# State space mixer: first inputs loaded during the output linear, a second Toeplitz buffer, the scale product inside the chain, the root spread by TensorE, states first

## The reference

```python
def rmsnorm(x, g):
    y = xf * lax.rsqrt(jnp.mean(xf * xf, axis=-1, keepdims=True) + EPS)
    return y.astype(x.dtype) * g
...
x = x + gate * y            # odd_mix: y = (...) @ w_out
return rmsnorm(x, final_g)
...
# s5_mixer: 64 groups of 16 channels, 64 complex states each
bu_re = jnp.einsum('blgh,gph->lbgp', u, bb_re)
bu_im = jnp.einsum('blgh,gph->lbgp', u, bb_im)
_, _, s_re, s_im = lax.associative_scan(
    _ssm_combine, (a_seq_re, a_seq_im, bu_re, bu_im), axis=0)
y = (jnp.einsum('lbgp,ghp->blgh', s_re, c_re) - jnp.einsum('lbgp,ghp->blgh', s_im, c_im))
y = y.reshape(bsz, seq, D_MODEL) + d_skip * x
h = jax.nn.gelu(y)
val, gate = jnp.split(h @ w_glu, 2, axis=-1)
z = val * jax.nn.sigmoid(gate)
return (z @ w_out).astype(x.dtype)
```

## Time and profile before

| | us |
|---|---|
| median of 3 runs | 4361.92 |
| lowest and highest | 4359.04, 4365.49 |
| the profiled execution | 4365.49 |
| its span | 4363.6 |
| TensorE busy | 4080.8 (94%) |
| VectorE, ScalarE, GpSimd busy | 2007.1 (46%), 1271.8 (29%), 1308.2 (30%) |

### The profile page before, as it was taken

The page is one execution under the profiler, slowest core; times in us unless marked ns, Lnnn a source line. Parts: engine busy times, 40 slices in busy tenths (PEclk is TensorE's granted clock), DMA queues, the critical chain, the costliest instruction groups (busy, mean ns, idle before and its releaser), DMA issues.

```text
span 4363.6 us, 51384 instructions
## 1 busy us (share of the span) xinstructions
PE 4080.8 (94%) x20067; PEld 3122.6 (72%) x20067; DVE 2007.1 (46%) x2419; ACT 1271.8 (29%) x1884; POOL 1308.2 (30%) x780
## 2 busy tenths in 40 slices
PE   7999998899999999779999999999999899999998
PEld 5776774458777774568888888876666678888886
DVE  4264662765676775561453233324444554323322
ACT  3122320212222221231232232224545543223222
POOL 1530000021111110012344444443344444444443
PEclk8999999999999999899999999999999999999999
DMA  6111004331222223751223333321000032333333
GB/s 230 39 37 55 0 0 143 139 131 64 73 79 73 79 86 131 162 139 49 81 92 97 99 98 96 100 88 68 25 20 25 20 107 92 96 98 100 96 97 105
DMA packets 120619, 372.02 MB, mean 85 GB/s; under 512 B 18004, under 2 KB 35727, under 8 KB 116688
## 3 DMA queue, kind: packets, MB, share of 16 engines
q1 hardware_dynamic: 102496, 300.84, 22.1%
q0 software_dynamic: 11584, 55.30, 3.4%
q10 hardware_dynamic: 6384, 13.70, 0.8%
HBM read 329.37 MB, written 38.06 MB: 84 GB/s over the span
## 4 chain that ended last, share of the span: by engine, by line
PE 62%; issue 17%; DVE 8%; POOL 6%; DMA 3%; ACT 2%; SPq 1%; POOLq 0%; ACTq 0%; DVEq 0%
PE banks L274 22%; PE banks L3037 6%; POOL w_parts L259 6%; PE banks L1227 5%; PE banks L288 5%; PE banks L693 5%; PE banks L1602 4%; PE banks L979 3%; PE banks L3111 2%; DVE neg_max L1058 2%; PE banks L3140 1%; PE banks L3127 1%; PE banks L1583 1%; DMA w_ring<-in_weights 1%; PE banks L1633 1%
## 5 line engine op out<-in xcount | busy, mean ns | idle before, releaser
L259 POOL TENSOR_TENSOR w_parts<-w_ring,w_parts 128x1024 fp32r<-128x1024 f32 x344 | 835.5, 2430 | 1143.3 <-ACT w_parts L252 1143.3
L274 PE MATMUL banks<-x_high,w_parts 128*128 128x512 f32 x2944 | 912.3, 390 | 0.0
L252 ACT ACTIVATE w_parts<-w_ring 128x1024 fp32r<-128x1024 f32 x344 | 364.5, 1060 | 1298.1 <-PE banks L274 1280.8
L274 PEld LDWEIGHTS banks<-x_high,w_parts 128*128 128x128 f32 x2944 | 552.6, 188 | 116.8 <-issue 2.1
L274 PE MATMUL banks<-x_low,w_parts 128*128 128x512 f32 x1472 | 572.8, 389 | 0.0
L274 PE MATMUL banks<-hidden_high,w_parts 128*128 128x512 f32 x1600 | 482.3, 391 | 6.0 <-POOL w_parts L259 6.0
L3245 DVE TENSOR_TENSOR_SCAN arena<-arena,flags 128x128 f32<-128x128 f32 (+3 forms) x192 | 229.6, 1200 | 285.7 <-ACT arena L3186 284.3
L274 PEld LDWEIGHTS banks<-hidden_high,w_parts 128*128 128x128 f32 x1600 | 301.8, 189 | 70.9 <-POOL w_parts L259 6.8
L2929 DVE TENSOR_TENSOR hidden_high<-banks,gate_temps 128x512 f32 (+1 forms) x88 | 60.9, 692 | 571.9 <-PE banks L274 571.8
L274 PEld LDWEIGHTS banks<-x_low,w_parts 128*128 128x128 f32 x1472 | 276.3, 188 | 59.2 <-issue 1.9
L1227 PE MATMUL banks<-parts_b,w_ring_low 128*128 128x512 f32 x896 | 303.9, 406 | 14.5 <-DVE resid_low L391 9.7
(11 more groups left out here) (448 smaller groups left out, 6495.6 us busy)
## 6 DMA issues: line engine op xcount, KB each, us to landing
w_ring<-in_weights SPq DMA_DIRECT2D x488, 512.0 KB, 3.5
arena<-in_hy_dft SPq DMA_DIRECT2D x11, 1536.0 KB, 6.1
s_cl<-arena POOLq DMA_DIRECT2D x4, 1152.0 KB, 5.4
arena<-s_cl POOLq DMA_DIRECT2D x4, 1152.0 KB, 7.0
resid<-in_xT ACTq DMA_DIRECT2D x2, 2048.0 KB, 25.9
resid<-in_xT POOLq DMA_DIRECT2D x1, 4096.0 KB, 13.7
arena<-in_fn_seq POOLq DMA_DIRECT2D x1, 4096.0 KB, 18.0
resid_spill<-resid POOLq DMA_DIRECT2D x1, 4096.0 KB, 12.6
```

Source lines behind the costliest of these rows:

```text
L252: nc.scalar.activation(WP[:, g % 2, 0, :], WR[:, (g % RING) * TILE:(g % RING + 1) * TILE], ACT.Identity).then_inc(w_hi, 1)
L259: nc.gpsimd.tensor_tensor(WP[:, g % 2, 1, :], WR[:, (g % RING) * TILE:(g % RING + 1) * TILE], WP[:, g % 2, 0, :].bitcast(F32), ALU.subtrac ...
L274: mm = nc.tensor.matmul(PS[:, bank + h // H, :], w[a][:, k % KB, :], srcs[b][:, k, at + h:at + h + H], start=(first and i + q == 0), stop= ...
```

## The change

- Quarter 0 of the inputs is loaded into its own place `U0` by GpSimd during the output linear, as soon as it has been written to `u_dram`; `normed(0)` reads it from there. SyncE begins with `inputs_in(1)`. `U0` shares its place with `STT_`, whose first column VectorE now clears.
- The Toeplitz matrices get a second buffer `TP[1]`, at the place of HT's last two blocks, cleared once the spill has landed. Toeplitz copies run up to one quarter ahead. A third powers buffer `CLS[2]` lies in HT too, `CLS[3]` is `CLS[1]` again.
- `normed(q+1)` stands inside `chain(q)`, behind the four products that read the banks.
- The taps move ahead on TensorE (`taps`): quarter 0 around the token sums in `OdOut`, quarter 1 behind `states_in(0)`, quarter 2 behind `results(0)`, quarter 3 ahead of `results(2)`. ScalarE's order follows.
- The last square is added on VectorE, so TensorE sums one tensor. The sums of all tokens and their roots for `RINV` go away; `spread_rows` spreads `RINV8` over the partitions by 8 matmuls within `results(3)`, and ScalarE copies them into `RINV`.
- GpSimd brings back the results of quarters 0 to 2; SyncE issues half of the last result copy, ScalarE the other half; the residual comes back after the last result.

```diff
+    CLS += [HT_[:, 3840:6144].rearrange(cl_shape["pattern"], i=2, j=QP, n=9), CLS[1]]
-    TP = ar(27136, 2048, "p (g n) -> p g n", g=16)
+    TP = [t.rearrange("p (g n) -> p g n", g=16) for t in (ar(27136, 2048), HT_[:, 6144:8192])]
+    U0 = ar(25072, 2048, "p (g c) -> p g c", g=16)
...
 OdOut.pool
-            nc.gpsimd.memset(TP, 0.0).then_inc(s5_zero, 1)
-            nc.gpsimd.memset(STT_, 0.0).then_inc(s5_zero, 1)
+            nc.gpsimd.memset(TP[0], 0.0).then_inc(s5_zero, 1)
+            g.wait_ge(u_out, 16)
+            for t in range(CK):
+                g.dma_start(U0[16 * t:16 * t + 16], u_dram[0:2 * P, t, :].rearrange("(g h) c -> h g c", h=16)
+                            ).then_inc(s5_e, 16)
...
 OdOut.pe
+            wait_done(p, OdOut.done)
+            S5.taps(p, 0, range(4))
             p.wait_ge(s5_vbt, 4)
             p.wait_ge(s5_zero, 2)
...
+            OdOut.waits(p, "sq_free", 7)
+            for t in range(CK):
+                mm = nc.tensor.matmul(PS[:, 4, 0:NC], PARTS_OF_ONES[:, 112 - 16 * t:240 - 16 * t], ACC_SQ[:, t:T:CK],
+                                      start=(t == 0), stop=(t == CK - 1))
+            mm.then_inc(n_sem["spread_in"], 1)
+            S5.taps(p, 0, range(4, QP))
...
 S5.sp
             def toeplitz(q):
                 s.wait_ge(s5_km, 4 * (q + 1))
+                s.wait_ge(s5_zero, 3 if q == 0 else 5)
+                if q > 1:
+                    s.wait_ge(s5_y, 4 * (q - 1))
                 if q:
-                    s.wait_ge(s5_y, 4 * q)
+                    s.wait_ge(s5_tp, 16 * CK * q)
                 for t in range(CK):
...
-            inputs_in(0)
+            inputs_in(1)
             inputs_out(3)
...
             toeplitz(0)
-            s.wait_ge(spilled, 80)
+            inputs_in(2)
+            toeplitz(1)
+            inputs_in(3)
             for q in range(4):
                 s.wait_ge(s5_ye, 4 * (q + 1))
...
+                    s.wait_ge(y_out, 16 * CK * q)
+                for t in range(CK if q < 3 else CK // 2):
+                    S5.result_out(s, q, t)
+                if q < 2:
+                    toeplitz(q + 2)
+            s.wait_ge(y_out, 16 * CK * 4)
+            s.dma_start(HT[:, 6:8, :], y_dram[6 * P:8 * P].rearrange("(k p) t c -> p k (t c)", p=P)).then_inc(x_home, 16)
+            s.wait_ge(x_home, 16)
             s.dma_start(XT, spill).then_inc(x_home, 16)
...
 S5.pool
             magnitudes(0)
+            g.wait_ge(spilled, 80)
+            g.wait_ge(s5_r, 8)
+            powers_in(2)
+            nc.gpsimd.memset(TP[1], 0.0).then_inc(s5_zero, 1)
             g.wait_ge(s5_vt, 8)
             magnitudes(1)
...
+            g.wait_ge(s5_st, 1)
+            phases_in(2)
+            magnitudes(2)
+            result_in(0)
+            g.wait_ge(s5_st, 2)
+            phases_in(3)
+            magnitudes(3)
+            g.wait_ge(s5_y, 8)
+            powers_in(3)
+            result_in(1)
+            result_in(2)
...
 S5.chain
             nc.vector.memset(FLAG[:, 0:1], 0.0).then_inc(s5_vr, 1)
+            if q < 3:
+                S5.normed(v, q + 1)
...
 S5.dve
-            normed(0)
-            normed(1)
-            v.wait_ge(s5_zero, 4)
+            S5.normed(v, 0)
+            v.wait_ge(s5_un, 1)
+            link(nc.vector.memset(STT_[:, :, :, 0:1], 0.0))
             v.wait_ge(u_out, 64)
...
 S5.act
             kernels(0)
...
+            kernels(1)
+            for q in range(3):
+                S5.turned_out(a, q + 1)
+                if q == 2:
+                    kernels(3)
                 results(q)
...
+                if q == 0:
+                    kernels(2)
+            a.wait_ge(s5_st, 3)
+            for k in (0, 1):
+                high(k)
+            a.wait_ge(s5_v, 4)
+            a.wait_ge(s5_tp, 16 * CK * 4)
+            for j in (-2, -1):
+                round_ahead(a, PLAN["glu"], j)
+            for k in (2, 3):
+                high(k)
+            OdOut.waits(a, "spread_in", 2)
+            nc.scalar.activation(RINV[:, :].rearrange("p (c t) -> p t c", t=CK),
+                                 PS[:, 0:2, :].rearrange("p b (t c) -> p (b t) c", c=NC),
+                                 ACT.Identity).then_inc(n_sem["root"], 1)
+            results(3)
             a.wait_ge(s5_ye, 16)
+            a.wait_ge(y_out, 16 * CK * 3)
+            for t in range(CK // 2, CK):
+                S5.result_out(a, 3, t)
             for k in range(4, KB):
                 high(k)
...
 S5.pe
-            OdOut.waits(p, "root", 3)
             states_in(0)
-            wait_done(p, OdOut.done)
-            kernels(0)
+            S5.taps(p, 1, range(QP))
             for q in range(4):
                 if q < 3:
                     p.wait_ge(s5_vr, q + 1)
                     S5.turned(p, q + 1)
                     states_in(q + 1)
+                if q == 2:
+                    S5.taps(p, 3, range(QP))
                 results(q)
-                if q < 3:
-                    kernels(q + 1)
+                if q == 0:
+                    S5.taps(p, 2, range(QP))
```

More of the change, by code:

```diff
@@ L2233, in act @@
                                  ).then_inc(n_sem["root"], 1)
-            OdOut.waits(a, "mean_in", 1)
-            for h in range(2):
-                nc.scalar.activation(RINV[:, h * H:(h + 1) * H], PS[:, 6 + h, :], ACT.Sqrt, scale=1.0 / D,
-                                     bias=EPS(RMS_EPS)).then_inc(n_sem["root"], 1)
         def dve(v, link):
@@ L2255, in _build @@
     S.append(OdOut)
[L2256 removed]
+    for _key, _n in (("sq_ready", 8), ("sq_free", 7), ("spread_in", 2), ("root", 2), ("scaled", KB)):
         n_count[_key] += _n
@@ L2429, in dve @@
                 low(k)
-            OdOut.waits(v, "root", 3)
-            link(nc.vector.reciprocal(RINV[:, :], RINV[:, :]))
-            v.wait_ge(x_home, 16)
+            OdOut.waits(v, "root", 2)
+            v.wait_ge(x_home, 32)
             for k in range(KB):
```

168 lines of the change are left out of this document (75 added, 93 removed).

## The result

| | before | after |
|---|---|---|
| median, us | 4363.57 (4 runs, 4359.04 to 4365.49) | 4333.98 (4 runs, 4331.79 to 4335.03) |
| ratio after to before | | 0.9933, 95% interval 0.9916 to 0.9950 |
| the profiled execution, its span | 4365.49, 4363.6 | 4331.79, 4329.7 |

The change saves 29.6 us by the medians, 0.68%. The forecast was 37.3 us less, 4324.6 us, with a range of 4313 to 4338. The result lies in that range, but above the 4319 to 4331 that the prediction gave to its main theory.

A forecast was written before the change was run, and what follows sets the result against it. No engine is busy throughout the mixer's 150 us; head, middle and tail carry it. Savings of 11.0 + 11.1 + 14.5 + 0.7 = 37.3 us take the median 4361.92 to 4324.6 us, range 4313 to 4338.

The forecast's parts named there:

- main theory: The summed forecast for the mixer stage, with (c) included: total of 4319 to 4331 us, chance 0.66.
- (a): Middle of the mixer: DMA engines or SyncE bound the quarters, which stay at 26.4 us; 12.6 us more, 4337; chance 0.14.
- (d): ScalarE closes a circle, evicting taps q only after Toeplitz copy q-1 lands: 38.7 us a quarter, total 4374; chance 0.03.
- (e): Head: U0 lands after the output linear; up to 11 us less gained, 4336; chance 0.04 together with smaller losses.
- (c): TensorE is late at the low clock, 26.9 us a quarter against 22.2; +4.7 us, 4329; counted within the forecast's 0.66.
- (b): Chain 0 starts earlier, divided issue saves 2.7 us: 4319, down to 4314 if the tail's blocks pass sooner; chance 0.12.
- Start of chain 0: Head: early U0 load lets chain 0 start once the last inputs land, 1790.7 instead of 1801.7; 11.0 us saved.
- the slack that I gave ScalarE: Head: ScalarE's wait for Toeplitz copy 0, landing by 1792 to 1797, costs nothing, with 10 us to the next chain.
- The four chains: Middle: VectorE's four chains run back to back, 86.3 us against 97.4; 11.1 us saved.
- End of the chains to the last GELU: Behind the last chain only the state part of results 3 and GELUs are left; 14.5 us saved.
- the term "5.1 us": Time from the last chain's end to the last GELU, with a handover, against 19.6 us before.
- The tail: Last GELU to the reload's issue: ScalarE issues four of eight copies; 0.7 us saved, 2.7 if issuing takes the time.

The follow-up runs named there:

- the late load: Changed kernel, but GpSimd loads quarter 0 into U0 only after the output linear has ended, ahead of the spill; stage 149.36 us, total 4335.86 us.
- the first experiment: Changed kernel, but GpSimd waits for the end of the last chain before making the low weight parts of the GLU's first tiles; stage 139.03, total 4331.67 us.
- the combined kernels: Changed kernel with late spill, late GpSimd weight parts, 4 useless matmuls, earlier input evictions: 4322.28 us; second also puts quarter 2's taps behind its states: 4322.89 us.

## Why the prediction was right, and where not

**Direction and range** came out as forecast, the size 6.4 us too large in the stage (30.85 against 37.3). The mechanism of each step is in the trace: the late landing at the head, chains back to back, the Toeplitz copy off the tail, the reload 6.4 us behind the last GELU. Rivals (a), (d) and (e) didn't happen: no chain waited for states, ScalarE closed no circle. That the total, 4334.0, lies near the 4337 of (a) is chance, and direction and range alone don't show the terms right. Of (c) only the low clock ahead of the last GELU came, and not because TensorE was late. The hope of (b) that the last blocks pass sooner without the 4 MB reload beside them did not come true: they took 8.45 us before and 8.43 after.

**Start of chain 0**, 9.5 instead of 11.0: the step that takes the landing over as 16.4 us was mis-sized, it took 18.2. What decides was named rightly: the spill moved away brings it 7.4 us earlier. The spill is not all of it, as the late load shows (19.7 us). That the place of `normed(1)` costs and saves nothing by itself was right within 0.3 us. The slack that I gave ScalarE was wrong: Toeplitz copy 0 landed so that the eviction ran at 1800.57, not by 1792 to 1797, because I took the 7 us of an issue in free queues for one in the crowd, 13.25 us. States 1 ended at 1810.5 and chain 0 at 1811.9; 1.4 us of slack were left of my 10.

**The four chains**, 90.0 instead of 86.3: the step that failed is "back to back", a sum over VectorE's own durations with nothing beside it. I had checked who waits for the chain, not what runs next to it. The change moves GpSimd's two subtractions of the GLU's weight parts, which were long behind the chains (1907.7 against 1899.1), into chain 3. They need ScalarE's roundings, and those moved ahead of results 3 (1865.89); in GpSimd's queue they now stand behind the reload of result 2, issued at 1871.34 when that result had landed, and start right behind it. Two VectorE operations grew by 2.0 us each, shown by moving the subtractions away. The Trainium skill's page "SBUF — State Buffer", section "SBUF: two separate sides", has the rule: VectorE and GpSimd share a pair of SBUF ports under an exclusive lock, which a VectorE operation with two SBUF inputs takes against a GpSimd one that reads SBUF. The trace agrees, 3.25 instead of 1.23 us, and the subtractions lost time too, 6.13 instead of 4.69; by that rule the forecast would have been up to 4.7 us higher, the time of the two subtractions (an estimate, from 4.69 us before). In different runs the hit was none (where the subtractions came behind the chain), one operation by 2.0 us, two by 2.0 each, or one by 4.5 to 4.9. The trace of before already had a case of it: in chain 0 the scans took 5.27 us beside a copy of GpSimd, in chain 1 4.62 without one:

```profile
1809.26 5.27 DVE L2387 TENSOR_TENSOR_SCAN arena<-squares,arena 128x1024 f32<-128x1024 f32 x2
...
1810.63 1.75 POOL L2333 COPY arena<-arena 128x1024 f32<-128x1024 f32 x1 [30.14 <-PE banks L2496]
...
1831.75 4.62 DVE L2387 TENSOR_TENSOR_SCAN arena<-arena 128x1024 f32<-128x1024 f32 x2
```

**End of the chains to the last GELU**, 12.2 instead of 14.5: the term "5.1 us" was taken from quarter 0 of before. It holds, 5.0 us, when TensorE has work ahead of it, and is 7.3 when it has waited 11.8 us. My sum priced a low clock for TensorE when busy and forgot it where it is idle. The rows of before had it: the first part of results 3 took 6.03 us behind 9.67 us of idle time and that of results 0 6.30 behind 10.42 (the prediction, which writes "up to 6.03", misread the larger of the two); with the first part moved ahead, the same loss falls on the state part.

**The tail**, 1.7 instead of 0.7: the division of the issues gave 1.6. The Trainium skill's page "DMA: Bandwidth & Descriptors", section "Issuing engines are not separate DMA queues", allows no more than the sequencer's time. The trace agrees: eight issues took 5.48 us, and the gain stayed below the 2.7 that half of them would give. The end of tile 0 also depends on the clock. From the landing to its end both 8.4 and 9.5 us occur:

```profile
1897.80:1906.30 8.50, 5.29 (x17) 3.89 (x17) 3.82 (x2) 3.84 (x3) 0.00 (x0) 0.79 0.87 322
```

```profile
1899.70:1909.30 9.60, 5.62 (x13) 4.51 (x14) 3.81 (x2) 3.81 (x3) 0.00 (x0) 0.65 0.87 327
```

(windows of the changed kernel and of the first experiment.) The clock of the whole stretch, 0.79 and 0.65, is not what decides: before it was 0.60, and the stretch took 8.45 us. The clock of the last matmuls does: from TensorE's start on the last block to the end of tile 0 it is 4.5 us at 0.67 in the changed kernel and 4.5 at 0.66 before, but 5.6 at 0.50 in the first experiment. Seven of the eleven experiments have the longer one, at 0.50 to 0.52, the others 4.6 to 4.8 us at 0.62 to 0.64. Why a kernel falls on one side or the other was not found.

The prices don't add up to the gain: second buffer 13.0, order of the taps 5.7, early load 7.1 at the head, place of the product 0.3, division 1.6, reciprocals 0. They were taken by undoing one part each in one run each, two of them (buffer and order) remove the same wait, and in both GpSimd's subtractions missed the chain, which hides up to 4 us of their price. What stays open: in the combined kernels, whether a load of powers takes 13 us because of the small packets in SyncE's queue or of the queue that GpSimd issues on. I didn't try a load of the powers at another place.

The best kernels measured are the two combined ones (medians 4322.3 and 4322.9 us, ranges 4318.4 to 4332.0) and the changed kernel with the late spill (one run, 4320.3), about 0.9 to 1.1% below before and 0.3% below the changed kernel.

## What to carry to other kernels

When a step is moved off the critical path, ask what moves with it. Here two subtractions for the next stage slid beside the chain that had just become the bound, and the work that now stands first behind TensorE's idle time was 60% slower for it. A price read from a quieter stretch (7 us to issue a copy) is a lower bound for the same step in a crowd (13 us here): give slack that rests on it twice the room. When a part is undone to price it, compare the whole chain of terms, not the one start that moved: chain 0 started 2.6 us later with the products outside, and the last chain ended at the same time but for 0.3 us. And look for the largest transfer that nobody waits for soon: delaying the spill by one wait took 8.9 us off the stage, in these comparisons more than any part of the change but the second buffer.

## What the runs showed of the hardware

- Eight DMA issues of SyncE for the same copy took 7.06 us in a quieter stretch, 13.25 us beside a 4 MB spill and 8.52 us in the same place with the spill moved away; the issuing queue itself is held up.
- A transfer of 1 MB from SBUF to DRAM landed in 16.4 and 18.2 us with the spill beside it, in 11.9 us without, and in 19.7 us without the spill but with another 1 MB load beside it; the load of the powers of quarter 2, 1.15 MB, landed in 9.0 to 13.4 us in the changed kernel and its variants, where 7.0 is the median of such loads over the kernel before.
- Behind 11.8 us of idle time TensorE's granted clock was 0.60 over the next 6.2 us, and 64 small matmuls took 6.16 us; behind 4.3 us of idle time (late spill) they took 5.47, behind matmuls or 1.9 us of idle time 3.84.
- Two GpSimd subtractions of 128x1024 took 4.69 us before, 6.13 beside VectorE's last chain and 7.84 beside its low parts; the VectorE operations beside them took 3.25 instead of 1.23. In two runs (the products outside, the reciprocals put back) a VectorE operation began at most 0.4 us ahead of the first subtraction; there both subtractions ran in 4.65 and 4.64 us, and that one operation lasted 6.12 and 5.74.
